# A projection kernel's later quarters: x loaded as columns, and one turned tile of reciprocal roots in place of eight turned tiles of x

## The reference, cut to what matters

```
u    = x * rsqrt(mean(x * x, axis=-1) + 1e-6) * pre_norm      # per token, then a gain per feature
proj = u @ w_in                                               # 1024 x D_in, split into q, k, v, gates
...                                                           # three attention groups, gates
out  = x + rms_norm(concat(groups) @ w_out, post_norm)
```

## Time and profile before

| | |
|---|---|
| time, median of 3 runs | 2166.37 us (2165.32 to 2173.78) |
| the profiled execution | 2168.64 us, of which the span from first to last instruction is 2166.5 us |
| mean granted TensorE clock | 0.968 |
| TensorE busy with matmuls | 2062.5 us, 95% of the span |
| VectorE, ScalarE busy | 1553.7 us (72%), 1352.1 us (62%) |
| the projection stage | from the start to about 1030 us of the span |

### The profile page before, as it was taken

The page is one execution under the profiler, slowest core; times in us unless marked ns, Lnnn a source line. Parts: engine busy times, 40 slices in busy tenths (PEclk is TensorE's granted clock), DMA queues, the critical chain, the costliest instruction groups (busy, mean ns, idle before and its releaser), DMA issues. The chain is left out here.

```text
span 2166.5 us, 39340 instructions
## 1 busy us (share of the span) xinstructions
PE 2062.5 (95%) x12892; PEld 1725.8 (80%) x12892; DVE 1553.7 (72%) x4410; ACT 1352.1 (62%) x3520; POOL 115.4 (5%) x116
## 2 busy tenths in 40 slices
PE   6999899999999999999899999999999998899998
PEld 4788678888888888888787888887778887688886
DVE  6564684546564575346588999899799997888887
ACT  7454454545654464333798989899689998433333
POOL 1232310000000000002000000000000000000000
PEclk7999999999999999999799999899999999999999
DMA  4476666777576757679678577596769995245543
GB/s 157 154 242 213 190 216 196 237 214 219 161 230 205 238 184 232 224 240 288 164 145 167 110 153 150 105 176 130 156 155 215 231 270 171 93 160 174 173 157 115
DMA packets 351736, 401.40 MB, mean 185 GB/s; under 512 B 105616, under 2 KB 255248, under 8 KB 346688
## 3 DMA queue, kind: packets, MB, share of 16 engines
q1 hardware_dynamic: 343120, 364.80, 61.4%
q0 software_dynamic: 8432, 34.30, 5.1%
HBM read 255.62 MB, written 143.39 MB: 184 GB/s over the span
## 5 line engine op out<-in xcount | busy, mean ns | idle before, releaser
L854 PE MATMUL p_ps<-p_u_hi,p_w_hi 128*128 128x512 f32 x1344 | 535.2, 398 | 24.2 <-DVE p_p_c L739 10.4
L856 PE MATMUL p_ps<-p_u_hi,p_w_lo 128*128 128x512 f32 x1344 | 527.1, 392 | 0.0
L855 PE MATMUL p_ps<-p_u_lo,p_w_hi 128*128 128x512 f32 x1344 | 526.7, 392 | 0.0
L570 DVE TENSOR_TENSOR p_w_lo<-p_w_raw,p_w_hi 128x512 fp32r<-128x512 f32 x336 | 244.3, 727 | 335.7 <-ACT p_w_hi L423 334.1
L1621 ACT ACTIVATE probs<-probs,a_stat 128x256 f32<-128x256 f32 (+1 forms) x896 | 434.0, 490 | 49.9 <-DVE a_stat L1455 46.6
L423 ACT ACTIVATE p_w_hi<-p_w_raw 128x512 fp32r<-128x512 f32 x336 | 210.7, 627 | 331.2 <-PE p_ps L856 309.9
L854 PEld LDWEIGHTS p_ps<-p_u_hi,p_w_hi 128*128 128x128 f32 x1344 | 254.7, 190 | 83.6 <-issue 11.9
L856 PEld LDWEIGHTS p_ps<-p_u_hi,p_w_lo 128*128 128x128 f32 x1344 | 254.4, 189 | 54.4
L1455 DVE CUSTOM_DVE_ANT_0 probs<-a_ps_s,fixed 128x256 f32<-128x256 f32 (+1 forms) x704 | 251.3, 396 | 64.2 <-PE a_ps_s L1354 63.0
L855 PEld LDWEIGHTS p_ps<-p_u_lo,p_w_hi 128*128 128x128 f32 x1344 | 255.0, 190 | 50.8
L1408 PE MATMUL a_ps_o<-a_pT,a_v 128*64 128x128 f32 x3320 | 257.7, 286 | 22.8 <-ACT a_pT L1645 21.0
(11 more groups left out here) (202 smaller groups left out, 2760.8 us busy)
## 6 DMA issues: line engine op xcount, KB each, us to landing
p_w_raw<-in_w_in SPq DMA_DIRECT2D x156, 256.0 KB, 3.7
p_w_raw<-scratch_w_s SPq DMA_DIRECT2D x144, 256.0 KB, 3.8
scratch_qk_hi<-p_out_a SPq DMA_DIRECT2D x80, 256.0 KB, 4.0
scratch_qk_lo<-p_out_b SPq DMA_DIRECT2D x80, 256.0 KB, 4.1
a_v<-scratch_v SPq DMA_DIRECT2D x40, 512.0 KB, 7.5
scratch_gate<-p_out_a SPq DMA_DIRECT2D x64, 256.0 KB, 4.0
scratch_v<-p_out_a SPq DMA_DIRECT2D x256, 64.0 KB, 2.3
a_gate<-scratch_gate SPq DMA_DIRECT2D x64, 256.0 KB, 5.9
```

What stands on the lines that cost most here:

```text
L570: nc.vector.tensor_tensor(w_lo[:, m % 3, :, :], w_raw[:, entry(j, g), :, :], w_hi[:, m % 3, :, :].bitcast(F32), ALU.subtract).then_inc(w_l ...
L854: nc.tensor.matmul(bank, hi, u_hi[j][:, k, :], start=j < 2 and k == 0, stop=False, skip_group_check=True)
L855: nc.tensor.matmul(bank, hi, u_lo[j][:, k, :], start=False, stop=False, skip_group_check=True)
L856: last = nc.tensor.matmul(bank, lo, u_hi[j][:, k, :], start=False, stop=k == KH - 1, skip_group_check=True)
```

## The change

From the second quarter on, `raw` is filled with x itself, not with normalised values, by two loads of 2 MB (`load_columns`, issued by GpSimd) from a second, turned copy of x among the inputs (`x_columns`); the rows are still loaded to `x_next`, for the squares only. `scale` is gone for these tiles. In its place VectorE copies the reciprocal root of each token over 128 columns (`widen`, slot j = 1), TensorE turns this one tile, and VectorE multiplies (`normalize`, j = 4) eight pieces of `raw` of 128x128 in place: by the turned roots, read from PSUM, and by the gain of the feature, a value per partition. `x_next` is free once tile n-1 is squared, and GpSimd's wait says so. The first quarter is made as it was.

The two loads of a quarter stand in GpSimd's queue a pair apart. For the second quarter they stand behind the weight sums of pairs 1 and 2; for the third and the fourth in pairs i = 0 and i = 1 of the quarter before, ahead of nothing but the next loads of x. The first waits until the last `low_u` of the quarter has read `raw`, the second for the first to land. The counts of `ahead.w_loaded`, which they raise, are moved where it is awaited later.

```diff
@@ -94,6 +94,7 @@
         out_b = sb("out_b", [P, 3, CHUNK])
         turned = sb("turned", [P, CHUNK])
         p5_c22 = sb("p5_c22", [P, CHUNK])
+        spread = sb("spread", [P, P])
         ps = ctx.enter_context(nc.psum_tensor("p_ps", [P, 6, CHUNK], F32))
         ps_t = ctx.enter_context(nc.psum_tensor("p_ps_t", [P, 2, CHUNK], F32))
 
@@ -529,8 +530,6 @@
                         n = (quarter + 1) * XT + t
                         if j == 1:
                             root(n)
-                        if j == 2:
-                            scale(n, x_next)
                     if quarter == 3 and i == 1:
                         if j == 2:
                             act.wait_ge(mem_loaded, 32 + 16)
@@ -582,7 +581,7 @@
                     n = sum_number(quarter, name)
                     if name == "T1":
                         dve.wait_ge(raw_ready, XT * (quarter + 1))
-                        dve.wait_ge(u_turned, XT * (quarter + 1))
+                        dve.wait_ge(squared if quarter else u_turned, XT * (quarter + 1))
                     else:
                         dve.wait_ge(added, n)
                     if name in ("T2", "T4"):
@@ -606,6 +605,22 @@
                     t = n % XT
                     nc.vector.tensor_tensor(raw[:, t // 4, :, (t % 4) * P:(t % 4 + 1) * P], src.rearrange("p a (k n) -> p (a k) n", n=P),
                                             gain[:].unsqueeze(2).broadcast_to([P, KD, P]), ALU.mult).then_inc(raw_ready, 1)
+
+                def widen(n):
+                    dve.wait_ge(inverted, n + 1)
+                    dve.wait_ge(u_turned, n)
+                    nc.vector.tensor_copy(spread[:], ss[:, n % 2, 3:4].broadcast_to([P, P])).then_inc(scaled, 1)
+
+                def normalize(n, roots):
+                    dve.wait_ge(u_turned, n + 1)
+                    quarter, t = divmod(n, XT)
+                    if t % 4 == 0:
+                        dve.wait_ge(ahead.w_loaded, 32 * quarter - 16 + 4 * t)
+                    for k in range(KD):
+                        place = raw[:, t // 4, k, (t % 4) * P:(t % 4 + 1) * P]
+                        last = nc.vector.scalar_tensor_tensor(out=place, in0=roots, scalar=gain[:, k:k + 1], in1=place,
+                                                              op0=ALU.mult, op1=ALU.mult)
+                    last.then_inc(raw_ready, 1)
 
                 def low(g, block):
                     dve.wait_ge(a_ready, A_NO[g, block] + 1)
@@ -744,7 +759,7 @@
                     x21, x22 = w_out[:, KH:, 0:CHUNK], w_out[:, KH:, CHUNK:]
                     of, x, y = ((spare[:], x12, x11), (x12, x22, x12), (spare[:], x22, spare[:]), (x21, x21, spare[:]))[n]
                     if n == 0:
-                        dve.wait_ge(ahead.w_loaded, 16 * KD)
+                        dve.wait_ge(ahead.w_loaded, 96 + 16 * KD)
                         dve.wait_ge(m_stored, 48)
                     else:
                         dve.wait_ge(ahead.w_made, n)
@@ -781,8 +796,9 @@
                             mean(n)
                         if j == 1:
                             invert(n)
+                            widen(n)
                         if j == 4:
-                            keep(n, ps_t[:])
+                            normalize(n, ps_t[:, 0, 0:P])
                     if quarter < 3 and i == NP - 2 and j in (1, 4):
                         add_u(quarter + 1, "T1" if j == 1 else "T3")
                     if quarter < 3 and i == NP - 1 and j - 1 in U_AT:
@@ -898,7 +914,7 @@
                         pe.wait_ge(scaled, n + 1)
                         pe.wait_ge(raw_ready, n)
                         wait_v(g)
-                        turn(n, x_next, ps_t, u_turned)
+                        nc.tensor.transpose(ps_t[:, 0, 0:P], spread[:], ident[:]).then_inc(u_turned, 1)
                     if quarter == 3 and i in (2, 3) and j == 3:
                         pe.wait_ge(scaled, TILES + i - 1)
                         pe.wait_ge(raw_ready, TILES + i - 2)
@@ -921,15 +937,26 @@
 
             @block.gpsimd
             def _(pool):
+                def load_columns(quarter, c):
+                    if c:
+                        pool.wait_ge(ahead.w_loaded, 32 * quarter - 16)
+                    else:
+                        pool.wait_ge(u_lo_ready, NJ * quarter)
+                    at = quarter * QT + c * CHUNK
+                    pool.dma_start(raw[:, c, :, :], io["x_columns"].rearrange("(k p) n -> p k n", p=P)[
+                        :, :, at:at + CHUNK]).then_inc(ahead.w_loaded, 16)
+
                 for g in range(-1, 3 * NP):
                     quarter, i = divmod(g, NP)
                     t = i + 1 - X_AT
                     if g >= 0 and 0 <= t < XT:
                         n = (quarter + 1) * XT + t
-                        pool.wait_ge(u_turned, n)
+                        pool.wait_ge(squared, n)
                         if t == 0:
                             pool.wait_ge(u_lo_ready, u_number(quarter, 1) + 1)
                         pool.dma_start(x_next, io["x"][bass.ts(n, P), :]).then_inc(x_next_loaded, 16)
+                    if i < 2 and g >= NP:
+                        load_columns(quarter + 1, i)
                     g += 1
                     if g >= NP:
                         continue
@@ -952,6 +979,8 @@
                     if g:
                         pool.wait_ge(w_lo_ready, number(g - 1, 5) + 1)
                     nc.gpsimd.tensor_tensor(s4, a12, s2, ALU.subtract).then_inc(w_added, 1)
+                    if g in (1, 2):
+                        load_columns(1, g - 1)
 
                 pool.wait_ge(multiplied, NJ * (3 * NP + 4) + 7)
                 for k in range(KD):
@@ -1906,7 +1935,7 @@
             def _(act):
                 act.wait_ge(early.consts_loaded, CONSTS)
                 rounds(act, scalar_round, lambda g: g.scalar_parts(act))
-                act.wait_ge(ahead.w_loaded, 16 * KD + 48)
+                act.wait_ge(ahead.w_loaded, 96 + 16 * KD + 48)
                 act.wait_ge(groups[1].values_done, groups[1].TOTAL)
                 nc.scalar.activation(ahead.w0_hi, ahead.b11, ACT.Copy).then_inc(ahead.w_hi_ready, 1)
 
@@ -2372,7 +2401,7 @@
                   for pair in PAIRS])
     by_part = lambda g: np.asarray(g).reshape(KD, P).T
     given = {
-        "x": np.asarray(x)[0][token_order()], "x_rows": np.asarray(x)[0][row_order()], "mem": np.asarray(mem)[0], "pre_gain": by_part(pre_norm), "w_in": w,
+        "x": np.asarray(x)[0][token_order()], "x_columns": np.asarray(x)[0][token_order()].T, "x_rows": np.asarray(x)[0][row_order()], "mem": np.asarray(mem)[0], "pre_gain": by_part(pre_norm), "w_in": w,
         "sink": np.asarray(sink_a), "mem_gain": by_part(mem_norm), "w_mem": np.asarray(w_mem_kv)[0],
         "w_out": np.asarray(w_out)[0], "post_gain": np.asarray(post_norm), **constants(),
     }
```

## The result

The changed kernel takes 2172.36 us, the kernel before 2167.79 us (medians of 20 runs each); the ratio is 1.0025, with a 95% interval from 1.0014 to 1.0037. It is some 5 us slower, within the 0.5% that stand for no change, where a gain of 12 us was forecast. The profiled execution takes 2175.55 us around a span of 2173.7 us.

What follows compares the result with a forecast made beforehand. The prediction took TensorE to bound quarters 1 and 2, and SyncE's stores and the weight sums a few stretches of quarter 0. 16.6 - 2.8 - 0.9 - 1.0 = 11.9 us gained, so 2155 us, range 2147 to 2164.

Steps and rivals of the forecast that it cites:

- Both signs that the prediction named for being wrong: A new wait of TensorE in quarters 1 and 2, or quarter 0 stalls grown by more than 4 us.
- TensorE's 16.6 us: Seven transposes fewer per tile take 0.69 us from TensorE's queue, 16.6 us over 24 tiles.
- VectorE's multiplications: Eight 128-column multiplications per tile in slot 4, put at 0.28 us each, 2.24 us together.
- The tight pairs i = 2 and 3: Tile pairs with rotary work ahead of the multiplications; the join before product 6 comes some 0.1 us late.
- The loads: Six new 2 MB loads: not waited for themselves, but able to slow others, chiefly over V's stores in quarter 0.
- I put 1 us on it, between 0 and 4: Price for quarter 0's second column load, over V's stores, possibly slowing the weight load of 107.86.
- GpSimd now waits for the squares ... so 0: GpSimd's queue moves on earlier, but in slow stretches it waits for weight loads anyway; priced at 0.
- What of the 16.6 us reaches the end: Quarters 1 and 2 keep their full 11.0 us; quarter 0 loses 2.8 us of its gain to stalls.
- I count four such tiles of eight: Quarter 0 tiles in front of stalls give up their gain: 2.8 us lost, at best none, at worst 5.5.
- 9 x 0.1 = 0.9 us: Late joins before product 6 in nine tiles of pairs i = 2, 3, 8: 0.9 us, between 0 and 5.
- Rival 1: Quarter 0's stalls swallow all eight tiles' gain and column loads cost 3 to 4 us; about 2160 us, 20%.
- rival 3: Column loads push weight loads behind V's stores past their use, in pair i = 1 of three quarters; about 2178, 5%.

Runs made afterwards that it cites:

- experiment 8: Kernel before, with one transpose in place of eight for tiles of quarters 2 and 3 alone (work left out); ratio 0.9951, median 2156.8 us.
- experiment 3: Changed kernel without any column loads or the wait for them (work left out); ratio to the kernel before 0.9989, median 2165.5 us.
- experiment 1: Changed kernel with GpSimd's wait ahead of the x rows put back to the turned tile; ratio to the kernel before 1.0002.
- experiment 10: Changed kernel without column loads and with GpSimd's x load behind the turn as before (work left out); ratio to the kernel before 0.9975, median 2160.9 us.
- experiments 5: Kernel before, with one of eight transposes per tile in all quarters, all else kept (work left out); ratio 0.9974, median 2158.2 us.
- 9: Repeat run: kernel before, with one of eight transposes per tile in all quarters (work left out); ratio 0.9957, median 2157.4 us.
- Experiments 6: The change for the x of quarters 2 and 3 alone, quarter 0 running as in the kernel before; ratio to the kernel before 0.9997.
- experiment 7: The change for x of quarters 2 and 3 alone, multiplications moved behind the join except in pair 6; ratio to the kernel before 0.9958.
- 14: The change for x of quarters 2 and 3 alone, multiplications behind the join except pair 6, weight sums stored by GpSimd; ratio to the kernel before 0.9949.
- 12: Whole change, multiplications behind the join except pair 6, x rows behind the first sum, second column load in three parts; ratio to the kernel before 0.9956.

## Why the prediction was wrong

Both signs that the prediction named for being wrong came: TensorE has new waits in quarters 1 and 2, and its waits in quarter 0 grew by 13.0 us, to 27.7.

**What held.** TensorE's 16.6 us: 18.7 us by busy time, and 0.74 us for each tile of quarter 1 in experiment 8 (19.94 to 19.20) where 0.69 was forecast. `scale` was worth nothing by itself. VectorE's multiplications, 0.28 us forecast, take 0.26: 2.07 us from 376.91 to 378.98 for eight. `widen` takes 0.23 us. The tight pairs i = 2 and 3 lose 0.15 us each (19.35 in place of 19.20) where 0.1 stood. The column loads of quarters 1 and 2 are not waited for. The Trainium skill, "VectorE: DVE Perf Modes", section on the TRN2 errata, has a formula for a float32 add that gives 0.29 us for 128 columns as an estimate; these multiplications take 0.26. The estimate of 0.056 us for a transpose by the same section is half of the 0.106 us that experiment 8 shows (0.74 / 7).

```profile
376.91 2.15 DVE L621 SCALAR_TENSOR_TENSOR p_raw<-p_ps_t,p_gain,p_raw 128x128 f32<-128x128 f32 x8
378.98 0.69 DVE L754 TENSOR_TENSOR p_p_c<-p_ps,p_p_c 128x512 f32<-128x512 f32 x1
```

**The step that failed first: "The loads", "I put 1 us on it, between 0 and 4".** It counted the transfer's own 6.7 us and found that the backlog is gone when the weight load of 107.86 starts. But that load does not keep its time, for two reasons that the sum left out. The first column load, given no price at all, makes the weights of pair 2 late, so that SyncE's queue is 3.3 us late when V's stores begin. And the load of 107.86 stands in that queue behind V's stores, which are held while the second columns travel (6.02 us for four in place of 2.19). Taking the columns out gives quarter 0 10.9 us, and the kernel 6.8 us by the medians (experiment 3). With that belongs **"GpSimd now waits for the squares ... so 0"**: with the columns present it costs 5.6 us in quarter 0 and 1.4 in quarters 1 and 2 (experiment 1). By the marks of quarter 0 columns and wait together cost 8.8 us (experiment 10), less than 10.9 and 5.6; by the medians they add up (6.8 and 4.5 us alone, 11.4 together). So that split stays open.

**The second: "What of the 16.6 us reaches the end", "I count four such tiles of eight".** 2.7 us were to be gained in quarter 0 (5.5 less 2.8). The medians of experiments 5, 9 and 8 (2158.2 and 2157.4 with the saving in quarter 0, 2156.8 without) show no gain, and the marks of 5 and 9 show 5.6 and 2.6 us lost, more than "at worst all eight" allowed. With the quicker turn the ring of weight loads and sums takes 20.0 to 21.0 us a round, longer than TensorE's old 19.94, so TensorE runs ahead only to stand longer at pair V. The sum had read quarter 0 by its idle time, 8.8 us, and taken the full stretches as TensorE's alone; behind them the ring had next to no time to spare.

**The third, a mis-sized term: "9 x 0.1 = 0.9 us".** It holds for i = 2, 3. For i = 8, where 0.1 was forecast, and i = 9, which was not on the list, TensorE waits 0.70 to 0.76 us for the joins. Rotary work on L has one more copy, which the sum took from the pair of the earlier trace rows. Experiments 6 and 7 put the price in two quarters at 4.8 us.

**The balance**, by the marks: quarter 0 +13.6 (+4.8 left without columns and changed wait, experiment 10, and +8.8 for these two), quarters 1 and 2 -6.0 (-11.2 as in experiment 7, +4.8 for the joins, 0.4 unexplained); with the 1.7 us by which the first mark is late and a tail 2.1 us shorter, +7.2 us of span. The medians say +4.6, the ratio's interval 3.0 to 8.0. Rival 1 had the right place and mechanism but was bounded at zero gain; rival 3 had the right mechanism, columns that delay weight loads behind V's stores, and named the stall to look for, but put the same stall in all three quarters. It came in quarter 0 alone: the marks of the two others have no stall of 1 us between them.

**The better versions.** Experiments 7 and 14 (quarter 0 left alone) and 12 (the whole change, rearranged) all stand at 0.995 to 0.996, 9 to 11 us under the kernel before; they can't be told apart. What stays open: whether the quicker tile alone costs quarter 0 time or only brings nothing, how that would split between the x rows beside the weights and the clock behind the longer stall, and whether it is the DMA engines' queues or the memory that hold V's stores; neither was tried by itself.

## What to carry to other kernels

A stretch in which the bounding engine is busy 100% can still have a second chain with nearly the same period behind it; look at when the inputs of the next round land, and only where they land early count a saving there in full. Price a new bulk load not by its own waiting reader but by the first short transfer that leaves while it travels, and by everything that queue issues behind it. When an instruction moves on VectorE ahead of something TensorE waits for, check each variant of the pair, not the one nearest at hand.

## What the runs showed of the hardware

- A 2 MB load in flight stretches the issue of other transfers, not only their landing: four 64 KB stores held SyncE's queue 6.02 us (2.19 before, 2.73 in experiment 3 without the load), and stores of 256 KB landed after 9.5 us (3.5 before, 3.8 in experiment 3).
- Behind a TensorE stall of 8.00 us the granted clock was 0.50 from 122 to 126 us, the 1.2 GHz level, and eight matmuls cost 1.5 us more; behind one of 4.38 us (235.17) it was 0.57 from 235 to 239 us; behind one of 1.60 us it stayed at 1.00.
- Multiplications of 128 columns with an operand in PSUM and a value per partition cost 0.26 us each by distance, while their group shows a mean duration of 340 ns.
